# Expert stage of a two-layer block: the query product moved behind the output product, with the norm factor applied to its results

## The reference, cut to what matters

```python
h = h + mixed @ w_out[l]                                   # "output product"
h = h + peer_ffn(rmsnorm(h, g_ffn_norm[l]), peer_wq[l], peer_keys[l], peer_u[l], peer_v[l])

def rmsnorm(x, g):
    y = x * lax.rsqrt(jnp.mean(x * x, axis=-1, keepdims=True) + NORM_EPS)
    return y * g

def one(xb):                                               # in peer_ffn, per group of tokens
    q = (xb @ wq).reshape(C, PEER_HEADS, 2, PEER_DK_HALF)  # "query product"
    s = jnp.einsum('chpd,hpnd->chpn', q, keys)             # scores against 2 x 8 sets of 128 keys
    sv, si = lax.top_k(s, K)                               # K = 16
    ...                                                    # best 16 of the sums, softmax g, indices eidx
    act = gelu(jnp.einsum('chkd,cd->chk', u_tab[eidx], xb))
    return jnp.einsum('chk,chkd->cd', g * act, v_tab[eidx])
```

## Time and profile before

| what | before |
|---|---|
| median of 3 runs | 3220.27 us (3216.92 to 3225.36) |
| the profiled execution | 3220.23 us |
| its span in the profile | 3218.4 us |
| PE busy | 3036.2 us (94%) |
| VectorE busy | 1806.9 us (56%) |
| ScalarE busy | 986.7 us (31%) |
| GpSimd busy | 820.2 us (25%) |
| mean granted TensorE clock | 0.95 of full |

### The profile page before, as it was taken

How to read it: one execution, slowest core, us unless ns; L and a number is a source line. 1 busy time by engine, 2 the same in 40 slices (tenths; PEclk the granted TensorE clock), 3 DMA queues, 4 the chain that set the end, 5 groups by cost and what they waited for, 6 DMA issues and landing times. The chain is left out here.

```text
span 3218.4 us, 39318 instructions
## 1 busy us (share of the span) xinstructions
PE 3036.2 (94%) x15134; PEld 2599.4 (81%) x15134; DVE 1806.9 (56%) x3169; ACT 986.7 (31%) x1560; POOL 820.2 (25%) x553
## 2 busy tenths in 40 slices
PE   7688799999999999999999999999988899899998
PEld 7454588989899999999999787888857889778886
DVE  6764439999998268778787573322041255432311
ACT  2334123333334322222222323222121365432222
POOL 3100220000000132111110554444421254444442
PEclk8867899999999999999999999999998798999999
DMA  3100225656565789888886222323322000122232
GB/s 122 33 1 1 86 81 165 214 161 208 167 207 170 238 318 325 313 283 311 309 309 231 78 99 79 101 96 100 97 91 72 13 1 1 66 84 93 97 98 74
DMA packets 192798, 450.10 MB, mean 140 GB/s; under 512 B 15924, under 2 KB 107956, under 8 KB 192356
## 3 DMA queue, kind: packets, MB, share of 16 engines
q1 hardware_dynamic: 174036, 378.37, 36.0%
q0 software_dynamic: 18432, 67.12, 5.9%
q10 hardware_dynamic: 144, 2.10, 0.2%
HBM read 386.11 MB, written 60.82 MB: 139 GB/s over the span
## 5 line engine op out<-in xcount | busy, mean ns | idle before, releaser
L257 ACT ACTIVATE w_hi<-w 128x1024 fp32r<-128x1024 f32 (+2 forms) x489 | 507.2, 1039 | 1365.8 <-PE peer_psum L304 521.8
L267 POOL TENSOR_TENSOR w_lo<-w,w_hi 128x1024 fp32r<-128x1024 f32 (+3 forms) x233 | 542.6, 2341 | 987.3 <-ACT w_hi L257 987.3
L267 DVE TENSOR_TENSOR w_lo<-w,w_hi 128x1024 fp32r<-128x1024 f32 x256 | 313.1, 1223 | 223.1 <-ACT w_hi L257 219.2
L302 PE MATMUL peer_psum<-xn_hi,w_hi 128*128 128x448 f32 (+1 forms) x1088 | 408.5, 375 | 12.6 <-DVEq L494 11.1
L304 PE MATMUL peer_psum<-xn_hi,w_lo 128*128 128x448 f32 (+1 forms) x1088 | 401.6, 369 | 0.0
L303 PE MATMUL peer_psum<-xn_lo,w_hi 128*128 128x448 f32 (+1 forms) x1088 | 401.4, 369 | 0.0
L302 PE MATMUL peer_psum<-peer_w_hi,w_hi 128*128 128x448 f32 x1024 | 374.7, 366 | 0.7 <-ACT peer_act_out L1421 0.7
L304 PE MATMUL peer_psum<-peer_w_hi,w_lo 128*128 128x448 f32 x1024 | 374.0, 365 | 0.0
L303 PE MATMUL peer_psum<-peer_w_lo,w_hi 128*128 128x448 f32 x1024 | 374.0, 365 | 0.0
L1281 POOL DMA_INDIRECT peer_gathered<-in_peer_u,peer_chosen_here x64 | 72.3, 1129 | 867.7 <-DMA peer_gate<-peer_gates_out 616.0
L302 PE MATMUL ffn_psum<-ffn_hn_hi,w_hi 128*128 128x512 f32 x704 | 275.0, 391 | 10.5 <-DVE ffn_hn_lo L558 6.6
(11 more groups left out here) (390 smaller groups left out, 5569.1 us busy)
## 6 DMA issues: line engine op xcount, KB each, us to landing
w<-in_peer_uT SPq DMA_DIRECT2D x128, 512.0 KB, 4.1
w<-in_peer_v SPq DMA_DIRECT2D x128, 512.0 KB, 5.4
w<-in_f_w_gu SPq DMA_DIRECT2D x88, 512.0 KB, 3.6
peer_act<-peer_act_out SPq DMA_DIRECT2D x128, 224.0 KB, 4.3
peer_gate<-peer_gates_out SPq DMA_DIRECT2D x14, 2048.0 KB, 10.1
peer_gates<-peer_gate SPq DMA_DIRECT2D x32, 896.0 KB, 6.3
peer_act_in<-peer_act SPq DMA_DIRECT2D x128, 224.0 KB, 4.0
w<-in_f_w_down SPq DMA_DIRECT2D x32, 512.0 KB, 3.5
```

The source lines that it names most:

```text
L257: act.activation(self.hi[:, x, 0:c], self.buf[:, x, 0:c], ACT.Copy).then_inc(self.rounded, 1)
L267: eng.tensor_tensor(self.lo[:, x, 0:c], self.buf[:, x, 0:c], self.hi[:, x, 0:c].bitcast(F32), ALU.subtract).then_inc(self.split, 1)
L302: pe.matmul(out, w[0], x[0], start=start, stop=False)
```

## The change

The query product runs right behind the output product, on rows that carry the gain and not the norm factor (`raw`). The factor is made meanwhile and multiplied into the query results by VectorE. The normalised rows `xn`, which only the U product and the last tokens need, are made by VectorE between the copies of the query results. `fn` becomes a `Late` that takes its buffers from outside. `places` is loaded later, since `raw` lies where it goes.

```diff
     # class Late
+    def high_on_act(self, act, to, j0=0, j1=None):
+        for j in range(j0, self.n if j1 is None else j1):
+            if self.need is not None:
+                act.wait_ge(self.need[0], self.need[1](j))
             act.activation(to.hi[:, j, :], self.src(j), ACT.Copy, scale=self.gain(j)).then_inc(self.high, 1)
...
     # peer: buffers
-        normed = (at("fn_sq", 20480, [P, 2, SEQ]), at("fn_rs", 24576, [P, SEQ]), at("fn_tmp", 28672, [P, 3, SEQ]))
+        raw = Split(at("raw_hi", 20480, [P, DT, SEQ], F32R), at("raw_lo", 36864, [P, DT, SEQ], F32R))
...
-        fn = Norm(st, "fn", lambda j: kit.real(j), None, DT, SEQ, EPS1, ..., split=(xn, lambda j: (slice(None), j)))
+        fn = Late(st, "fn", kit.real, DT, EPS1, lambda j: kit.gain("g_ffn_norm", j), ps[:, 4, :],
+                  need=(hsum, lambda j: j + 1), bufs=(Ao[:, 0:2, :], Ao[:, 2, :], total))
-        tiles += [tile(("q", n), lambda k: [xn.pair(slice(None), k)], need=(fn.out, lambda k: k + 1))
+        tiles += [tile(("q", n), lambda k: [raw.pair(slice(None), k)], need=(fn.split, lambda k: k + 1))
...
     # SP
-                sp.dma_start(keys ...).then_inc(side, 16)
-                sp.dma_start(places ...).then_inc(side, 16)
-                sp.dma_start(iota ...).then_inc(side, 16)
+                sp.dma_start(keys ...).then_inc(keys_in, 16)
+                sp.dma_start(iota ...).then_inc(places_in, 16)
+                lin.ring.load_to(sp, U0 + 3)
+                sp.wait_ge(q_copied, DT)
+                sp.dma_start(places ...).then_inc(places_in, 16)
                 lin.ring.load_to(sp, U0 + 5)
...
     # GpSimd
+                for n in range(DT):
+                    lin.ring.split_to(pool, n + 3)
+                    fn.on_pool(pool, n, n + 1)
                 lin.ring.split_to(pool, U0 + 2)
...
     # PE
-                lin.run(pe, lambda n: n < DT)
+                lin.run(pe, lambda n: n < DT + 2)
                 fn.on_pe(pe)
-                lin.run(pe, lambda n: n >= DT)
-                pe.wait_ge(side, 48)
+                lin.run(pe, lambda n: n >= DT + 2)
+                pe.wait_ge(keys_in, 16)
                 pe.wait_ge(q_copied, DT)
...
+                    if c == 0:
+                        pe.wait_ge(normed, DT)
...
     # ScalarE
-                lin.ring.round_to(act, DT)
-                fn.on_act(act, lambda: lin.ring.round_to(act, DT + 3))
                 for n in range(DT):
-                    slot, free = rounding(lin, act, ("q", n))
-                    act.activation(qT[:, n, :], slot[:, 0, :], ACT.Copy).then_inc(q_copied, 1)
-                    act.wait_ge(q_copied, n + 1)
-                    act.nop().then_inc(free, 1)
+                    lin.ring.round_to(act, n + 3)
+                    fn.high_on_act(act, raw, n, n + 1)
+                    fn.on_act(act, n, n + 1)
+                lin.ring.round_to(act, DT + 4)
+                fn.root_on_act(act)
+                lin.ring.round_to(act, U0 + 2)
...
     # VectorE, in the loop over the output tiles and behind it
+                    if n:
+                        fn.low_on_dve(dve, raw, n - 1, n)
-                fn.on_dve(dve, own)
-                dve.wait_ge(side, 48)
+                fn.low_on_dve(dve, raw, DT - 1, DT)
+                fn.root_on_dve(dve)
+
+                def norm_row(j):
+                    x = ntmp[:, j % 2, :]
+                    own.link(dve.scalar_tensor_tensor(out=x, in0=kit.real(j), scalar=kit.gain("g_ffn_norm", j),
+                                                      in1=fn.rs, op0=ALU.mult, op1=ALU.mult))
+                    own.link(xn.write_hi(dve, (slice(None), j), x))
+                    xn.write_lo(dve, (slice(None), j), x).then_inc(normed, 1)
+
+                for n in range(DT):
+                    slot, free = lin.arrived(dve, ("q", n))
+                    dve.tensor_tensor(qT[:, n, :], slot[:, 0, :], fn.rs, ALU.mult).then_inc(q_copied, 1)
+                    dve.wait_ge(q_copied, n + 1)
+                    dve.nop().then_inc(free, 1)
+                    if n < DT // 2:
+                        norm_row(2 * n)
+                        norm_row(2 * n + 1)
+                dve.wait_ge(normed, DT)
+                dve.wait_ge(places_in, 32)
```

More of the change, by code:

```diff
@@ L497, with __init__ @@
 class Late:
-    def __init__(self, st, name, src, n, eps, gain, ps, need=None, square_gain=None, like=None):
+    def __init__(self, st, name, src, n, eps, gain, ps, need=None, square_gain=None, like=None, bufs=None):
         self.kit, self.src, self.n, self.eps, self.gain = st.kit, src, n, eps, gain
         self.ps, self.need, self.square_gain = ps, need, square_gain
-        self.sq = st.sb(f"{name}_sq", [P, 2, SEQ]) if like is None else like.sq
-        self.rs = st.sb(f"{name}_rs", [P, SEQ])
-        self.total = st.sb(f"{name}_total", [P, SEQ])
+        if bufs is not None:
+            self.sq, self.rs, self.total = bufs
+        else:
+            self.sq = st.sb(f"{name}_sq", [P, 2, SEQ]) if like is None else like.sq
+            self.rs = st.sb(f"{name}_rs", [P, SEQ])
+            self.total = st.sb(f"{name}_total", [P, SEQ])
         self.squared = st.sem(f"{name}_squared")
@@ L549, in on_pe, with low_on_dve @@
         pe.matmul(self.ps, self.kit.ones[:, :], self.total[:, :], start=True, stop=True).then_inc(self.summed, 1)
-    def high_on_act(self, act, to):
-        for j in range(self.n):
+    def high_on_act(self, act, to, j0=0, j1=None):
+        for j in range(j0, self.n if j1 is None else j1):
+            if self.need is not None:
+                act.wait_ge(self.need[0], self.need[1](j))
             act.activation(to.hi[:, j, :], self.src(j), ACT.Copy, scale=self.gain(j)).then_inc(self.high, 1)
-    def low_on_dve(self, dve, to):
-        for j in range(self.n):
+    def low_on_dve(self, dve, to, j0=0, j1=None):
+        for j in range(j0, self.n if j1 is None else j1):
             dve.wait_ge(self.high, j + 1)
@@ L1142, in peer @@
         Ao = st.sb("act_out", [P, AS, SEQ])
+        total = nc.alloc_sbuf_tensor_at("peer_fn_total", [P, SEQ], F32, offset=io["mixT_at"] + 12288)
+        ntmp = nc.alloc_sbuf_tensor_at("peer_fn_tmp", [P, 2, SEQ], F32, offset=io["mixT_at"])
         a_dram = nc.dram_tensor("peer_act", (NK * P, DTOK), F32, kind="Internal").ap()
@@ L1146, in peer @@
         mix_split = st.sem("mix_split")
-        side = st.sem("side_loaded")
+        keys_in, places_in = st.sem("keys_loaded"), st.sem("places_loaded")
+        normed = st.sem("rows_normed")
         hsum = st.sem("residual_added")
@@ L1179, in peer @@
         summed = st.sem("gathered_sum_done")
-        fn = Norm(st, "fn", lambda j: kit.real(j), None, DT, SEQ, EPS1,
-                  lambda j: kit.gain("g_ffn_norm", j), ps[:, 4:5, :], 1, need=(hsum, lambda j: j + 1),
-                  bufs=normed, split=(xn, lambda j: (slice(None), j)))
+        fn = Late(st, "fn", kit.real, DT, EPS1, lambda j: kit.gain("g_ffn_norm", j), ps[:, 4, :],
+                  need=(hsum, lambda j: j + 1), bufs=(Ao[:, 0:2, :], Ao[:, 2, :], total))
         tiles = [tile(("o", n), lambda k: [mix.pair(slice(None), k)], need=(mix_split, lambda k: k + 1)) for n in range(DT)]
-        tiles += [tile(("q", n), lambda k: [xn.pair(slice(None), k)], need=(fn.out, lambda k: k + 1))
+        tiles += [tile(("q", n), lambda k: [raw.pair(slice(None), k)], need=(fn.split, lambda k: k + 1))
                   for n in range(DT)]
@@ L1220, in _ @@
             def _(sp):
-                sp.dma_start(keys[:, :, :], t["peer_keys"].rearrange("p (h n) -> p h n", h=PH)).then_inc(side, 16)
-                sp.dma_start(places[:, :, :], t["c_places"].rearrange("p (a n) -> p a n", a=TOPK)).then_inc(side, 16)
-                sp.dma_start(iota[:, :], t["c_iota"]).then_inc(side, 16)
+                sp.dma_start(keys[:, :, :], t["peer_keys"].rearrange("p (h n) -> p h n", h=PH)).then_inc(keys_in, 16)
+                sp.dma_start(iota[:, :], t["c_iota"]).then_inc(places_in, 16)
+                lin.ring.load_to(sp, U0 + 3)
+                sp.wait_ge(q_copied, DT)
+                sp.dma_start(places[:, :, :], t["c_places"].rearrange("p (a n) -> p a n", a=TOPK)).then_inc(places_in, 16)
                 lin.ring.load_to(sp, U0 + 5)
```

## The result

| | before | after |
|---|---|---|
| median | 3218.6 us (3216.61 to 3225.38, 6 runs) | 3202.95 us (3195.57 to 3208.58, 6 runs) |
| ratio | | 0.9934, 95% interval 0.9912 to 0.9956 |
| profiled execution | 3220.23 us | 3196.9 us |
| its span | 3218.4 us | 3195.1 us |

The change made the kernel faster by 0.5 to 0.7%: the two medians differ by 15.65 us (their quotient is 0.9951), and the ratio on record, 0.9934, stands for 21 us; its interval takes in both. The median after lies inside the range and 4 us above the forecast of 3198.6.

The account below looks back on a forecast made before the run. TensorE is busy nearly everywhere, so only its idle or slow stretch between output and query product counted; 25.1 us, cut to 21.6 by VectorE's split stalls, took 3220.23 to 3198.6 us, range 3191.5 to 3206.5.

Parts of the forecast that it names:

- PE idle between the products, a half clock behind it and seven sums: Between output and query product: removing these on PE alone gains about 24.1 us.
- The late last result: Ahead of the scores: five GpSimd splits hold VectorE's row blocks, 10.6 us; last query result 3.5 us later than PE allows.
- the sum: Forecast total: scores start at about 425.85 instead of 447.46, 21.6 us gained, carried one for one to the end.
- Rival 1: Query results: VectorE is not held up by splits, last copy follows PE; 25.1 us gained, 3195.1 us; chance 0.10.
- q3's bank: Last query tile q7 takes this PSUM bank, copied at 416.8, 0.8 us after PE is ready for it.
- rival 2: Clock falls ahead of the scores after 3.55 us idle; PE loses 2.6 us, 19.0 gained, 3201.2 us; chance 0.18.
- the likeliest case: Whole kernel: 21.6 us gained without a clock fall, 3198.6 us, or 3197 to 3200; chance 0.55.
- The argument by nearness: Ahead of the scores: 3.55 us idle is nearer 3.39 (full rate after) than 3.99 (not), so no clock fall.
- The feed: Weight rounding and splitting for query tiles: split 5.6 us after the tile before, needed after 10.9; hidden, costs nothing.
- SP: Loads of `places` and tiles 19 and 20 behind the last copy arrive in time: zero, at worst 1.5 us.
- Rivals 3, 4 and 5: Gain partly lost behind scores (8 to 18 left, 0.09); no shift, about 3219 to 3221 (0.05); slower through SP's queue (0.03).

Follow-up runs that it names:

- dve_splits: Changed kernel with the weight splits of tiles 13 to 17 moved from GpSimd to VectorE; scores at 45.7 us, top-k at 56.0 us behind the last output matmul's start.
- The control: The changed kernel run again, unchanged, beside a group's variants; ratio 0.9914 against the kernel before in the first group.
- again_2: The changed kernel unchanged, a third time, in a later group; ratio 0.9936 against the kernel before, span 3209.1 us.
- sum_alone: Changed kernel with the query product still waiting for normalised rows, only the sum moved beside the output product; ratio 1.0005 against the kernel before.
- before_again: The kernel before, unchanged, profiled once more in one execution; span 3226.8 us, top-k at 81.0 us behind the last output matmul's start.

## Why the prediction was right

**The place and the mechanism.** PE idle between the products, a half clock behind it and seven sums were to be gained, 24.1 us (by the prediction's own times of q7 it is 24.3); 24.2 were. The late last result was named with its cause: five splits, five stretched operations. I had put them at 2.0 to 2.2 us each, 10.6 in all; they were 2.08, 2.09, 1.30, 2.08 and 2.13, 9.7 in all. They fell on row blocks 0, 2, 4, 5 and 7, where I had 0, 2, 3, 5 and 6. So the scores came 22.6 us sooner, where the sum said 21.6. Rival 1, by which VectorE is not held up, did not come about. The Trainium skill, page "SBUF — State Buffer", section "SBUF: two separate sides", says that GpSimd and a VectorE operation with two SBUF inputs take turns on one port pair, which the one that comes first holds for its whole instruction. The traces agree: all five long operations ended 0.54 to 0.56 us behind their split, wherever in it they began, and in dve_splits none was over 0.75 us. PE did not wait for q3's bank, where the prediction had 0.8 us: it was copied by 409.7, 0.4 us ahead of need.

**The size that was off** is the clock ahead of the scores. The sum took no fall, "since 3.55 is nearer to 3.39", and gave the fall a chance of 0.18 and a cost of 2.6 us. It fell in all three profiles of the changed kernel, behind 3.27 to 3.29 us of idle, and cost 4.1 to 4.3 us. That is rival 2, so the likeliest case of the prediction, with a chance of 0.55, is not what happened. The price was too low because the half clock lasted longer: the prediction took 5.2 us of it, to the end of the earlier trace rows, and in the changed kernel's three profiles it lasted 9.0 to 9.3 us from the scores' start. In the stage that the earlier trace rows come from it did end soon behind those rows, 5.4 us behind the first matmul:

```profile
1792.00:1793.00 1.00, 1.00 (x4) 0.75 (x4) 0.00 (x0) 0.57 (x2) 0.25 (x1) 0.66 0.00 0
1793.00:1794.00 1.00, 1.00 (x6) 0.81 (x5) 0.00 (x0) 0.00 (x0) 1.00 (x2) 1.00 0.00 0
```

Why it lasted longer ahead of the expert product was not tried. With both sizes corrected the gain is 22.6 - 4.2 = 18.4 us, or 3201.8 for the profiled execution; the median after is 3202.95, and that of before moved to 3218.6. The argument by nearness was bad, as the last section shows.

**What was luck.** The two errors point in opposite ways: the splits cost 0.9 us less than the sum had, and the clock 4.2 us more. The forecast of 21.6 us gained is 3.1 us off the stretch's 18.5. That the time still lies well inside the range is owed to the range, which was made to take in rival 2 and the scatter.

**The feed, SP, the stages behind.** No wait for a weight came up in the query tiles; `places` landed 3.8 us behind its issue and the two weights behind it in 5.0 each, and the top-k came 14.5 us behind that issue. Rivals 3, 4 and 5 did not come about: from the top-k on, the changed kernel's three profiles have 2761.7, 2772.2 and 2775.5 us, the kernel before 2760.7 and 2774.3.

**The scatter.** I took it from three runs (8.4 us). The control's own four runs span 3192 to 3214, which is why parts of 4 to 7 us had to be read in the stretches.

## What to carry to other kernels

When a vector engine's work is moved into the shadow of the matmuls, add to it the time of the GpSimd operations that it meets: here each of five splits of 2.4 us cost it 1.3 to 2.1 us, which turned a shadow into the last thing waited for. Ask when the scalar that starts that work can be had: moving one sum of 1 us one tile forward brought 6.8 us to the next stage, without another instruction. A wait of 3.3 us of PE ahead of the scores cost 4.1 to 4.3 us more by the clock, more than its length. And a change of 0.2% is read in the stretch it touches, between two marks that both kernels have.

## What the runs showed of the hardware that I had not expected

**The same idle time lets the clock fall in one execution and not in the next.** First matmul of the first feed-forward stage, the changed kernel's first profile and its third (again_2):

```profile
1948.77 0.47 PE L302 MATMUL ffn_psum<-ffn_hn_hi,w_hi 128*128 128x512 f32 x1 [3.39 <-DVE ffn_hn_lo L563]
```

```profile
1961.42 0.77 PE L302 MATMUL ffn_psum<-ffn_hn_hi,w_hi 128*128 128x512 f32 x1 [3.40 <-DVE ffn_hn_lo L563]
```

The idle time before the stage `short` (3.99 to 4.02 us) was followed by 0.77 in the kernel before and in again_2, and by 0.47 in the changed kernel's first profile. Over all 14 profiles, 3.39 to 3.40 us of idle was followed by 0.47 in eight and by 0.64 to 0.77 in six, and 3.99 to 4.02 us by 0.47 in five and by 0.54 to 0.77 in nine. Shorter idle times did not spare the clock: it fell in three of three behind 3.27 to 3.29 us ahead of the scores, and within the 2.78 us ahead of the product with the ones in `sum_alone`. So the earlier trace rows, two single cases of 3.39 and 3.99, said nothing of 3.55. Three of three may be chance too; what ties the fall to a place is open.

**The V product has two speeds.** 100 us of it in the first profile of the kernel before and in before_again, the same program:

```profile
1400.00:1500.00 100.00, 100.00 (x495) 92.67 (x494) 74.90 (x105) 21.69 (x22) 14.93 (x16) 1.00 0.83 290
```

```profile
1400.00:1500.00 100.00, 100.00 (x486) 90.83 (x485) 73.14 (x104) 21.32 (x21) 15.00 (x16) 1.00 0.82 282
```

They show 495 matmuls or 486 in 100 us, at a granted clock of 1.00 both times and with PE busy throughout. The stretch from the top-k to the residual add goes with it in all 14 profiles: 1320 to 1321 us in the four with 495, 1332 to 1335 us in the ten with 485 or 486. Both kernels showed both values. The first output matmul came at 326.5 or 331.8 us in the kernel before and at 326.0 or 332.0 in the changed one, with a mean granted clock over the first 327.5 us of 0.77 or 0.78 for the early and 0.76 for the late ones; over all profiles it lies between 325.6 and 333.8. The last stretch varies by 6 us as well (1438.3 to 1444.7). These parts, the V product's first of all, make up the difference between executions outside the changed stretch; what sets them was not tried.
